# Turning values and decayed keys to token rows on VectorE instead of TensorE, in the head stage of a hybrid decoder layer

## The chip, the cores and the metric

The kernel runs on one core of a Trainium2 chip. The metric is the device time of one execution in microseconds, the median of several runs. One execution is also taken by the hardware profiler; its span (first to last instruction) and its rows are what the argument goes by.

## The reference

One step of a decoder layer with two branches over the same normalised tokens: HGRN2, a gated linear recurrence, and sliding-window attention. There are 1024 prompt tokens and 8 x 4 sample tokens, 1056 columns in all. The change lies in the recurrence, 8 heads of key and value width 128, computed chunk by chunk:

```python
b = jnp.cumsum(logf, axis=1)
...
o = jnp.einsum('bhts,bshv->bthv', att, v) + jnp.einsum('bthk,bhkv->bthv', q * jnp.exp(b), S)
b_last = b[:, -1]
k_dec = k * jnp.exp(b_last[:, None] - b)
S_new = jnp.exp(b_last)[..., None] * S + jnp.einsum('bshk,bshv->bhkv', k_dec, v)
```

q, k, v and the gates come from one projection of the tokens (1024 to 8448 columns). `k_dec` is the decayed key. Both `att @ v` and `k_dec^T v` sum over tokens, so v and `k_dec` are needed with tokens on the partitions.

## The kernel before

**Tiling.** The 1056 token columns are three slots of 352. A block is one 128-column tile of a weight matrix times all tokens; a slot of a block (L959, `slot`) is 24 matmuls into the PSUM bank `pj[g]`: eight tiles of the model width, each in three passes (weight high part with token high part, high with low, low with high), since fp32 is split into two fp32r parts. ScalarE makes a weight tile's high part (`split_hi`, L624), GpSimd its low part (`split_lo`, L554), SP loads it (`load`, L385) once the buffer is free. Projected blocks come out with channels on the partitions and tokens in the columns.

**The head stage.** It runs heads 0 to 7 (`head` on each engine, with a loop for 1 to 6). In head i, block 0 is the head's values, blocks 1, 2 and 3 are the next head's f, q and z, so that the next head's gates are computed meanwhile. Every engine has its order written out by hand, and the counts of its steps are kept by name in `Steps` tables (`act`, `dve`, `pe`, `pool`), so `dve.at(now, "dkm")` is the value that VectorE's semaphore has when step `dkm` of this head is done.

TensorE's order in a head: block 0 in three slots; block 1 slot 0; the transposes of the values (`vt0`, `vt1`, `vts`, nine) and of the decayed keys (`kt0`, `kt1`, `kts`, nine) with the identity as the moving operand (`turn`, L1025); block 1 slot 1; the intra-chunk products p0 and p1 (L1056 to L1071), which wait for VectorE's `dkm`; block 1 slot 2; `ps` and the eight products u (L1080) of `k_tok` and `v_tok`, which are the chunks' state updates; block 2 slots 0 and 1; the outputs o and `os` (L1087 to L1099), which wait for `atts`; block 2 slot 2; the sample tokens' state updates `us`; block 3 slot 0; the sums of squares `ms`; block 3 slots 1 and 2.

VectorE's order: `ha`, the norm of the head before (L1469); `kD`, the decayed key (L1473); four products into `d64` and `d32` (L1476, L1477); `dqm`, `dkm`, `qIm` (L1479 to L1482); the copies of the turned keys from PSUM to `k_tok` (L1485, L1487); the rounded parts of the sample tokens' keys `k3_hi`, `k3_hi2`, `k3_lo` (L1489 to L1492); the chain of states s1 to s8 (L1499, L1506); the masked scores `att0`, `att1`, `atts`; then the next head's exponents and the gates.

ScalarE copies the value slots from `pj` to `vT` (L705), which frees the bank for block 1, computes the exponentials, copies the turned values to `v_tok` (L729, L731) and rounds the sample tokens' part twice (L733, L734), for which GpSimd waits before `v3_lo` (L573) and `vexp` (L575).

Of the kernel before, what the change touches and what calls it, by code (L numbers as in the profile page):

```python
# [33 lines left out]
ACT = mybir.ActivationFunctionType  # L34

P = 128
# [4 lines left out]
NS = NB * DEC  # L41
T = SEQ + NS
NC = SEQ // P
SLOTS = 3
W = T // SLOTS
# [46 lines left out]
def hybrid_step(nc, x_prompt, x_sample, state_hgrn, cache_k, cache_v, norm_in, w_in, lb_logits, a_gnorm,  # L92
# [21 lines left out]
    norms = ["rl0", "rl1", "rls", "rx"]  # L114
    exponentials = ["v0", "ebl", "ebs", "xkD", "v1", "x64", "x32", "v2", "xdq", "xdk", "xqI"]
    turned = ["vt0", "vt1", "vts", "v3_hi", "v3_hi2"]
    squares_of_head = ["sq0", "sh0", "sq1", "sh1", "sqs", "shs"]
# [17 lines left out]
    exponents = ["kf", "scan", "kDa", "kDs", "a64q", "a64k", "a32q", "a32k", "cs", "css", "xa", "xas", "xc"]  # L135
    products = ["kD", "m64q", "m64k", "m32q", "m32k", "dqm", "dkm", "qIm", "kt0", "kt1", "kts", "k3_hi", "k3_hi2", "k3_lo"]
    chain = [f"s{c}" for c in range(1, NC + 1)]
# [20 lines left out]
    ])  # L158
    head_products = ["vt0", "vt1", "vts", "kt0", "kt1", "kts", "p0", "p1", "ps", "u0", "u1",
                     "o0", "o1", "os", "us0", "us1", "ms0", "ms1", "mss"]  # L160
# [18 lines left out]
    with ctx:  # L179
# [7 lines left out]
        pj = [ctx.enter_context(nc.psum_tensor(f"pj{g}", [P, 512], F32)) for g in range(SLOTS)]  # L187
        ps_a, ps_b, ps_c, ps_d, ps_e = [ctx.enter_context(nc.psum_tensor(f"ps_{n}", [P, 512], F32)) for n in "abcde"]
# [10 lines left out]
        ident = sb("ident", [P, P])  # L199
# [25 lines left out]
        k = sb("k", [P, T], where=area)  # L225
# [327 lines left out]
        def _(g):  # L553
# [11 lines left out]
            def head(i):  # L565
                B, now = head_blocks(i), now_of(i)
                split_lo(B(0))
                split_lo(B(1))
                if is_first(i):
                    g.wait_ge(masks_loaded, 48)  # L570
                g.wait_ge(act_done, act.at(now, "v3_hi2"))

                g.tensor_tensor(v3[NS:2 * NS, :], v_tok[0:NS, NC, :], v3[0:NS, :].bitcast(F32), ALU.subtract).then_inc(pool_done, pool.tick(now, "v3_lo"))  # L573
                g.wait_ge(pool_done, pool.at(now, "v3_lo"))
                g.tensor_tensor(v_exp[:], v3[:].bitcast(F32).rearrange("p (o v) -> p o v", o=1).to_broadcast([3 * NS, NB, P]),  # L575
                                batch_m[:].rearrange("p (b o) -> p b o", o=1).to_broadcast([3 * NS, NB, P]),
                                ALU.mult).then_inc(pool_done, pool.tick(now, "vexp"))
                split_lo(B(2))

                g.wait_ge(pe_done, pe.at(now, "os"))  # L580
                g.tensor_tensor(s0[:], s0[:], E[:, NC:NC + NB].rearrange("p (b o) -> p b o", o=1).to_broadcast([P, NB, P]),  # L581
                                ALU.mult).then_inc(pool_done, pool.tick(now, "s0e"))
                split_lo(B(3))
                if is_last(i):
                    split_lo(B(4))
# [34 lines left out]
        def _(a):  # L620
# [65 lines left out]
            def head(i):  # L686
# [15 lines left out]

                def v_copy(g):
                    a.wait_ge(slot_done, B(0)[0] * 3 + (g + 1))
                    a.activation(vT[:, span(g)], pj[g][:, 0:W], ACT.Copy).then_inc(act_done, act.tick(now, f"v{g}"))  # L705

                def exp(name, need, out, src, scale=1.0):
                    a.wait_ge(dve_done, dve.at(prev, need))
                    a.activation(out, src, ACT.Exp, scale=scale).then_inc(act_done, act.tick(now, name))

                v_copy(0)
                if not is_first(i):
# [3 lines left out]
                exp("xkD", "kDs", kD[:], kD[:])  # L716
                v_copy(1)
                exp("x64", "a64k", d64[:], d64[:])
                exp("x32", "a32k", d32[:], d32[:])
                v_copy(2)  # L720
                split_hi(B(2))
# [4 lines left out]
                exp("xqI", "scan", qI[:], b[:])  # L726
                for n, (bank, cols) in enumerate(((ps_a, slice(0, 4)), (ps_b, slice(4, 8)))):
                    a.wait_ge(pe_done, pe.at(now, f"vt{n}"))
                    a.activation(v_tok[:, cols, :], bank[:].rearrange("p (c v) -> p c v", c=4), ACT.Copy).then_inc(act_done, act.tick(now, f"vt{n}"))  # L729
                a.wait_ge(pe_done, pe.at(now, "vts"))  # L730
                a.activation(v_tok[0:NS, NC, :], ps_e[0:NS, 0:P], ACT.Copy).then_inc(act_done, act.tick(now, "vts"))  # L731
                a.wait_ge(act_done, act.at(now, "vts"))
                a.activation(v3[0:NS, :], v_tok[0:NS, NC, :], ACT.Copy).then_inc(act_done, act.tick(now, "v3_hi"))  # L733
# [222 lines left out]
        def _(t):  # L956
# [63 lines left out]
            def head(i):  # L1020
# [3 lines left out]

                def turn(bank, at, src, cols, name):  # L1025

                    for j, c in enumerate(cols):
                        r = P if c < NC else NS
                        mm = nc.tensor.transpose(bank[0:r, at + j * P:at + (j + 1) * P], src[:, c * P:c * P + r], ident[:, :])
                    mm.then_inc(pe_done, pe.tick(now, name))  # L1030

                def gate_slot(k_block, name, by, g):

                    if last and k_block == 3:
                        return
                    step = f"k{g}" if last and k_block == 2 else f"{name}{g}"
                    t.wait_ge(by[0], by[1].at(now, step))
                    slot(B(k_block), g)

                for g in range(SLOTS):  # L1040
                    t.wait_ge(dve_done, dve.at(prev, f"z{g}"))
                    slot(B(0), g)
                gate_slot(1, "v", (act_done, act), 0)
                t.wait_ge(act_done, act.at(now, "v2"))
                turn(ps_a, 0, vT, range(0, 4), "vt0")
                turn(ps_b, 0, vT, range(4, 8), "vt1")
                turn(ps_e, 0, vT, [NC], "vts")

                t.wait_ge(dve_done, dve.at(now, "kD"))
                turn(ps_c, 0, kD, range(0, 4), "kt0")  # L1050
                turn(ps_d, 0, kD, range(4, 8), "kt1")
                t.wait_ge(act_done, act.at(now, "vts"))
                turn(ps_e, P, kD, [NC], "kts")
                gate_slot(1, "v", (act_done, act), 1)

# [5 lines left out]
                for n, bank in enumerate((ps_a, ps_b)):  # L1061
# [9 lines left out]
                    mm.then_inc(pe_done, pe.tick(now, f"p{n}"))  # L1071
                gate_slot(1, "v", (act_done, act), 2)

                t.wait_ge(act_done, act.at(now, "vts"))
                t.wait_ge(dve_done, dve.at(now, "kts"))
                nc.tensor.matmul(ps_e[0:NS, 256:256 + NS], dk[:, SEQ:T], dq[:, SEQ:T], start=True, stop=True).then_inc(pe_done, pe.tick(now, "ps"))
# [272 lines left out]
        def _(v):  # L1349
# [106 lines left out]
            def head(i):  # L1456
# [4 lines left out]
                def need(steps, sem_, name):  # L1461
                    v.wait_ge(sem_, steps.at(now, name))

                def done(name):
                    return dve.tick(now, name)

                if not is_first(i):
                    need(act, act_done, "rx")
                    tt(ha[:, bass.ds(i - 1, 1), :], ha[:, bass.ds(i - 1, 1), :], rs[:].rearrange("p (o t) -> p o t", o=1), ALU.mult).then_inc(dve_done, done("ha"))  # L1469
                v.wait_ge(dve_done, dve.at(prev, "q2"))  # L1470

                need(act, act_done, "xkD")
                tt(kD[:], kD[:], k[:], ALU.mult).then_inc(dve_done, done("kD"))  # L1473
                for h, d in ((64, d64), (32, d32)):
                    need(act, act_done, f"x{h}")
                    tt(d[:, :, 1, :], d[:, :, 1, :], q[:, 0:SEQ].rearrange("p (c s t) -> p c s t", s=2, t=h)[:, :, 1, :], ALU.mult).then_inc(dve_done, done(f"m{h}q"))  # L1476
                    tt(d[:, :, 0, :], d[:, :, 0, :], k[:, 0:SEQ].rearrange("p (c s t) -> p c s t", s=2, t=h)[:, :, 0, :], ALU.mult).then_inc(dve_done, done(f"m{h}k"))  # L1477
                need(act, act_done, "xdk")
                tt(dq[:], dq[:], q[:], ALU.mult).then_inc(dve_done, done("dqm"))  # L1479
                tt(dk[:], dk[:], k[:], ALU.mult).then_inc(dve_done, done("dkm"))  # L1480
                need(act, act_done, "xqI")
                tt(qI[:], qI[:], q[:], ALU.mult).then_inc(dve_done, done("qIm"))  # L1482
                for n, bank in enumerate((ps_c, ps_d)):
                    need(pe, pe_done, f"kt{n}")
                    v.tensor_copy(k_tok[:, 4 * n:4 * n + 4, :], bank[:].rearrange("p (c v) -> p c v", c=4)).then_inc(dve_done, done(f"kt{n}"))  # L1485
                need(pe, pe_done, "kts")
                v.tensor_copy(k_tok[0:NS, NC, :], ps_e[0:NS, P:2 * P]).then_inc(dve_done, done("kts"))  # L1487
                need(dve, dve_done, "kts")
                v.tensor_copy(k3[0:NS, :], k_tok[0:NS, NC, :]).then_inc(dve_done, done("k3_hi"))  # L1489
# [280 lines left out]
```

## Time and profile before

| | us |
|---|---|
| median of 3 runs | 1321.42 (1320.48 to 1322.83) |
| the profiled execution, its own time | 1320.63 |
| its span | 1318.8 |
| TensorE busy (matmul) | 1287.5 |
| VectorE busy | 594.2 |
| ScalarE busy | 517.5 |
| GpSimd busy | 260.9 |
| mean granted TensorE clock over the span | 0.984 |

The busy shares add up what each engine did over the whole span. The chain is the work that ended last, followed back from the last instruction; what is not on it can move within its slack without moving the end. The timeline gives each instruction's start and duration and, in brackets, how long the engine was idle before it and what released it. The heads 1 to 6 repeat one pattern, so the rows of one of them stand for the others.

### The profile page before, as it was taken

How to read it: one execution, taken by the hardware profiler on the slowest of the kernel's cores; microseconds unless marked ns; L12 is line 12 of the kernel's file. 1: busy time of each engine (PE TensorE's matmuls, PEld its weight loads, DVE VectorE, ACT ScalarE, POOL GpSimd, SP SyncE). 2: the span in 40 equal slices, each digit the busy share in tenths (PEclk: the TensorE clock that was granted, in tenths of full speed). 3: DMA queues.
4: the chain of work that ended last, by engine and by line, in shares of the span. 5: the costliest groups of instructions: out<-in, count | busy, mean ns of one | idle time of the engine just before them, and what ended most of it. 6: DMA issues, size and time to landing. Idle time of an engine off the chain costs nothing.

```text
span 1318.8 us, 23470 instructions
## 1 busy us (share of the span) xinstructions
PE 1287.5 (98%) x9148; PEld 1227.6 (93%) x9148; DVE 594.2 (45%) x1237; ACT 517.5 (39%) x1019; POOL 260.9 (20%) x119
## 2 busy tenths in 40 slices
PE   5999999999999999999999999999999899999998
PEld 4999999999999999999999999999999899999885
DVE  6645657574847465600000155555556202345132
ACT  7463535445353535511111255555554324114111
POOL 0222221222322222222222111111110121342000
PEclk9999999999999999999999999999999899999999
DMA  6212121202021221121112311111100312241330
GB/s 198 67 33 66 36 65 34 80 18 80 18 80 37 76 58 41 35 64 48 48 35 49 85 33 32 32 32 32 32 16 1 106 32 64 62 98 33 119 125 37
DMA packets 136750, 73.61 MB, mean 56 GB/s; under 512 B 37185, under 2 KB 133138, under 8 KB 136690
## 3 DMA queue, kind: packets, MB, share of 16 engines
q1 hardware_dynamic: 136706, 72.99, 20.0%
q8 instruction: 31, 0.51, 0.2%
q14 instruction: 13, 0.11, 0.0%
HBM read 63.77 MB, written 10.22 MB: 56 GB/s over the span
## 4 chain that ended last, share of the span: by engine, by line
PE 93%; DVE 3%; ACT 2%; DMA 1%; issue 1%; SPq 0%; POOL 0%; DVEq 0%; ACTq 0%
PE pj L968 67%; PE pj L984 3%; PE pj L1328 3%; DVE scores L1617 2%; PE ps_a L1328 1%; PE ps_e L1328 1%; PE ps_d L1098 1%; PE ps_a L1169 1%; PE ps_d L1208 1%; PE ps_e L1208 1%; PE ps_b L1196 1%; PE ps_d L1328 1%; PE ps_b L1328 1%; PE ps_c L1328 1%; PE ps_c L1080 1%; PE ps_c L1196 1%
## 5 line engine op out<-in xcount | busy, mean ns | idle before, releaser
L968 PE MATMUL pj<-xn_h,w_h 128*128 128x352 f32 x1704 | 565.5, 332 | 3.4 <-DVE xn_l L1384 1.9
L968 PE MATMUL pj<-xn_h,w_l 128*128 128x352 f32 x1704 | 554.3, 325 | 0.0
L968 PE MATMUL pj<-xn_l,w_h 128*128 128x352 f32 x1704 | 553.5, 325 | 0.0
L558 POOL TENSOR_TENSOR w_l<-w_raw,w_h 128x1024 fp32r<-128x1024 f32 x82 | 203.3, 2479 | 688.8 <-ACT w_h L630 688.8
L968 PEld LDWEIGHTS pj<-xn_h,w_h 128*128 128x128 f32 x1704 | 325.8, 191 | 12.7 <-ACT w_h L630 3.5
L968 PEld LDWEIGHTS pj<-xn_l,w_h 128*128 128x128 f32 x1704 | 326.4, 192 | 0.3
L968 PEld LDWEIGHTS pj<-xn_h,w_l 128*128 128x128 f32 x1704 | 325.6, 191 | 0.0
L630 ACT ACTIVATE w_h<-w_raw 128x1024 fp32r<-128x1024 f32 x82 | 86.4, 1054 | 114.7 <-PE pj L968 100.1
L1565 DVE TENSOR_TENSOR mg<-sg,pj 128x352 f32 (+1 forms) x24 | 12.4, 522 | 151.9 <-PE pj L968 150.4
L835 ACT ACTIVATE scores<-scores,stat 128x256 f32<-128x256 f32 (+1 forms) x128 | 61.4, 481 | 0.0
L968 PE MATMUL pj<-hl_l,w_h 128*128 128x352 f32 x168 | 54.2, 323 | 0.0
L968 PE MATMUL pj<-hl_h,w_l 128*128 128x352 f32 x168 | 54.2, 323 | 0.0
L968 PE MATMUL pj<-hl_h,w_h 128*128 128x352 f32 x168 | 54.0, 321 | 0.0
L1399 DVE TENSOR_TENSOR zs<-zs,pj 128x352 f32<-128x352 f32 x24 | 12.5, 521 | 79.7 <-ACT zs L661 79.7
L581 POOL TENSOR_TENSOR s<-s,E 128x1024 f32<-128x1024 f32 x8 | 15.2, 1900 | 158.0 <-PE ps_d L1098 158.0
L661 ACT ACTIVATE zs<-pj 128x352 f32<-128x352 f32 x24 | 11.2, 465 | 84.7 <-PE pj L968 84.7
L949 ACT ACTIVATE y_sq<-y_o 128x1024 f32<-128x1024 f32 (+1 forms) x9 | 9.5, 1061 | 79.5 <-DVE y_o L1709 79.5
L1404 DVE TENSOR_TENSOR xn_l<-hb,xn_h 128x1056 fp32r<-128x1056 f32 x8 | 10.4, 1304 | 64.1 <-ACT xn_h L669 64.0
L661 ACT ACTIVATE sg<-pj 128x352 f32<-128x352 f32 x24 | 10.9, 465 | 66.7 <-PE pj L968 66.7
L1607 DVE TENSOR_SCALAR scores<-scores,stat 128x256 f32<-128x256 f32 (+1 forms) x128 | 35.5, 342 | 1.1
L1528 DVE TENSOR_TENSOR sq_l<-vT,sq_h 128x512 fp32r<-128x512 f32 (+1 forms) x24 | 33.6, 1451 | 0.0
L1687 DVE TENSOR_TENSOR sgb<-sgb,pj 128x352 f32 (+1 forms) x24 | 12.5, 520 | 46.7 <-PE pj L968 38.0
(362 smaller groups left out, 2005.4 us busy)
## 6 DMA issues: line engine op xcount, KB each, us to landing
w_raw<-in_w_in_dram SPq DMA_DIRECT2D x132, 256.0 KB, 3.4
x_t<-in_x_prompt_dram SPq DMA_DIRECT2D x8, 512.0 KB, 8.5
s<-in_state_hgrn_dram SPq DMA_DIRECT2D x8, 512.0 KB, 4.2
out_dram<-s SPq DMA_DIRECT2D x8, 512.0 KB, 3.2
w_raw<-in_w_pa_dram SPq DMA_DIRECT2D x16, 256.0 KB, 3.0
w_raw<-in_w_pb_dram SPq DMA_DIRECT2D x16, 256.0 KB, 4.5
wo_raw<-in_w_out_dram SPq DMA_DIRECT2D x8, 512.0 KB, 3.8
x_o<-in_x_prompt_dram SPq DMA_DIRECT2D x8, 512.0 KB, 4.1
```

Source lines behind the costliest of these rows:

```text
L558: g.tensor_tensor(w_l[p][:], w_raw[p][:], w_h[p][:].bitcast(F32), ALU.subtract).then_inc(w_lo_ready, 1)
L630: a.activation(w_h[p][:], w_raw[p][:], ACT.Copy).then_inc(w_hi_ready, 1)
L661: a.activation(out[:, span(g)], pj[g][:, 0:W], ACT.Sigmoid).then_inc(act_done, act.tick(where, f"{name}{g}"))
L835: a.activation(scores[:, u, keys], scores[:, u, keys], ACT.Exp, bias=stat[:, 1, u:u + 1], accum_out=stat[:, 3, u:u + 1]).then_inc(act_done ...
L968: mm = nc.tensor.matmul(pj[g][:, 0:W], w[:, kt, :], x[:, kt, span(g)], start=(kt == 0 and m == 0), stop=(kt == KT - 1 and m == 2))
L984: mm = nc.tensor.matmul(pj[g][:, 0:W], w[:, kt, :], x[:, kt, span(g)], start=(kt == 0 and m == 0), stop=(kt == KT - 1 and m == 2))
L1196: mm = nc.tensor.transpose(bank[:, o:o + P], scores[:, 2 * n + h, w * P:(w + 1) * P], ident[:, :])
L1208: mm = nc.tensor.matmul(bank[rows_h, o:o + P], v_tk[:, n - 1 + w, rows_h], PT[:, n % 3, 2 * h + w, :], start=(w == 0 or n == 0), stop=(w = ...
L1328: mm = nc.tensor.matmul(bank_of(n, m)[0:r, :], x[:, kt, cols], wo_rhs(m, lo, kt), start=(kt == 0 and i == 0), stop=(kt == KT - 1 and i == 2))
L1528: tt(sq_l[:, part[n]], vT[:, part[n]], sq_h[:, part[n]].bitcast(F32), ALU.subtract).then_inc(dve_done, done(f"sl{n}"))
L1607: v.tensor_scalar(target[:, u, keys(u)], target[:, u, keys(u)], st[:, 4, u:u + 1], None, ALU.mult).then_inc(dve_done, dve.tick(now, f"n{u}"))
L1617: v.tensor_tensor_reduce(out=scores[:, u, lo:2 * P], in0=bank[:, o + lo:o + 2 * P], in1=bias[:, h, lo:2 * P], scale=1.0, scalar=-3e38, op0 ...
```

## The change

TensorE no longer transposes in a head. VectorE does it with its 32x32 block transpose. For each value slot `turn_values(g)` reads the eleven 32-column blocks of `pj[g]` and writes them into `v_tok`; for each of the four value groups `iv` and four token groups `jt` one instruction turns all blocks of the slot that belong to that pair (two or three). The decayed keys are turned from `kD` in SBUF to `k_tok` in the same way, eight or nine blocks an instruction. `turn_values(0)` stands before `kD`, `turn_values(1)` after it, `turn_values(2)` after the products into `d64` and `d32`, and the keys after `qIm`. The copies of value slots to `vT` and of turned values on ScalarE and of turned keys on VectorE fall away. Block 1's slots now wait for the last transpose of a value slot (`v0_33`, `v1_33`, `v2_33`), and `ps` and u wait for `v2_33` and `kt33`. GpSimd's `v3_lo` gets a further wait, on the low part of block 1's weights.

```diff
-    exponentials = ["v0", "ebl", "ebs", "xkD", "v1", "x64", "x32", "v2", "xdq", "xdk", "xqI"]
-    turned = ["vt0", "vt1", "vts", "v3_hi", "v3_hi2"]
+    exponentials = ["ebl", "ebs", "xkD", "x64", "x32", "xdq", "xdk", "xqI"]
+    turned = ["v3_hi", "v3_hi2"]
...
                 g.wait_ge(act_done, act.at(now, "v3_hi2"))
+                g.wait_ge(w_lo_ready, B(1)[0] + 1)
...
-                v_copy(0)
...
-                v_copy(1)
...
-                v_copy(2)
...
-                for n, (bank, cols) in enumerate(((ps_a, slice(0, 4)), (ps_b, slice(4, 8)))):
-                    a.wait_ge(pe_done, pe.at(now, f"vt{n}"))
-                    a.activation(v_tok[:, cols, :], bank[:].rearrange("p (c v) -> p c v", c=4), ACT.Copy).then_inc(act_done, act.tick(now, f"vt{n}"))
-                a.wait_ge(pe_done, pe.at(now, "vts"))
-                a.activation(v_tok[0:NS, NC, :], ps_e[0:NS, 0:P], ACT.Copy).then_inc(act_done, act.tick(now, "vts"))
-                a.wait_ge(act_done, act.at(now, "vts"))
+                a.wait_ge(dve_done, dve.at(now, "v2_33"))
...
-                gate_slot(1, "v", (act_done, act), 0)
-                t.wait_ge(act_done, act.at(now, "v2"))
-                turn(ps_a, 0, vT, range(0, 4), "vt0")
-                turn(ps_b, 0, vT, range(4, 8), "vt1")
-                turn(ps_e, 0, vT, [NC], "vts")
-
-                t.wait_ge(dve_done, dve.at(now, "kD"))
-                turn(ps_c, 0, kD, range(0, 4), "kt0")
-                turn(ps_d, 0, kD, range(4, 8), "kt1")
-                t.wait_ge(act_done, act.at(now, "vts"))
-                turn(ps_e, P, kD, [NC], "kts")
-                gate_slot(1, "v", (act_done, act), 1)
+                gate_slot(1, "v", (dve_done, dve), 0)
+                gate_slot(1, "v", (dve_done, dve), 1)
...
-                gate_slot(1, "v", (act_done, act), 2)
-
-                t.wait_ge(act_done, act.at(now, "vts"))
-                t.wait_ge(dve_done, dve.at(now, "kts"))
+                gate_slot(1, "v", (dve_done, dve), 2)
+
+                t.wait_ge(dve_done, dve.at(now, "v2_33"))
+                t.wait_ge(dve_done, dve.at(now, "kt33"))
...
+                def turn_values(g):
+
+                    v.wait_ge(slot_done, head_blocks(i)(0)[0] * 3 + (g + 1))
+                    blocks = pj[g][:, 0:W].rearrange("p (b t) -> p b t", t=32)
+                    n = W // 32
+                    for iv in range(4):
+                        for jt in range(4):
+                            first = (jt - n * g) % 4
+                            c = (n * g + first) // 4
+                            many = len(range(first, n, 4))
+                            v.transpose(v_tok[32 * jt:32 * jt + 32, c:c + many, 32 * iv:32 * iv + 32],
+                                        blocks[32 * iv:32 * iv + 32, first:n:4, :]).then_inc(dve_done, done(f"v{g}_{iv}{jt}"))
+
                 if not is_first(i):
                     need(act, act_done, "rx")
                     tt(ha[:, bass.ds(i - 1, 1), :], ha[:, bass.ds(i - 1, 1), :], rs[:].rearrange("p (o t) -> p o t", o=1), ALU.mult).then_inc(dve_done, done("ha"))
+                turn_values(0)
                 v.wait_ge(dve_done, dve.at(prev, "q2"))
 
                 need(act, act_done, "xkD")
                 tt(kD[:], kD[:], k[:], ALU.mult).then_inc(dve_done, done("kD"))
+                turn_values(1)
...
+                turn_values(2)
                 need(act, act_done, "xdk")
...
-                for n, bank in enumerate((ps_c, ps_d)):
-                    need(pe, pe_done, f"kt{n}")
-                    v.tensor_copy(k_tok[:, 4 * n:4 * n + 4, :], bank[:].rearrange("p (c v) -> p c v", c=4)).then_inc(dve_done, done(f"kt{n}"))
-                need(pe, pe_done, "kts")
-                v.tensor_copy(k_tok[0:NS, NC, :], ps_e[0:NS, P:2 * P]).then_inc(dve_done, done("kts"))
-                need(dve, dve_done, "kts")
+                need(dve, dve_done, "kD")
+                key_blocks = kD[:].rearrange("p (b t) -> p b t", t=32)
+                for ik in range(4):
+                    for jt in range(4):
+                        many = NC + (jt == 0)
+                        v.transpose(k_tok[32 * jt:32 * jt + 32, 0:many, 32 * ik:32 * ik + 32],
+                                    key_blocks[32 * ik:32 * ik + 32, jt:4 * NC + (jt == 0):4, :]).then_inc(dve_done, done(f"kt{ik}{jt}"))
+                need(dve, dve_done, "kt33")
```

## Rows read from the trace of the kernel before

**Rows 1.** The page: TensorE's share, and the chain by engine.

```profile
PE 1287.5 (98%) x9148; PEld 1227.6 (93%) x9148; DVE 594.2 (45%) x1237; ACT 517.5 (39%) x1019; POOL 260.9 (20%) x119
...
PE 93%; DVE 3%; ACT 2%; DMA 1%; issue 1%; SPq 0%; POOL 0%; DVEq 0%; ACTq 0%
```

**Rows 2.** The chain in one head: start us, us, engine, tile, line, count.

```profile
189.99 14.80 PE pj L968 x93
204.79 0.44 PE ps_a L1029 x4
...
206.83 3.93 PE pj L968 x24
210.76 0.61 PE ps_a L1060 x8
...
212.97 4.01 PE pj L968 x24
216.98 0.18 PE ps_e L1076 x2
...
219.14 7.64 PE pj L968 x48
...
232.34 5.49 PE pj L968 x24
```

**Rows 3.** VectorE's timeline in the same head: start us, us, engine, line, operation.

```profile
194.04 1.26 DVE L1469 TENSOR_TENSOR ha<-ha,qI 128x1056 f32 x1 [3.48 <-ACT qI L698]
196.40 2.28 DVE L1473 TENSOR_TENSOR kD<-kD,k 128x1056 f32<-128x1056 f32 x1 [1.10 <-ACT kD L709]
198.64 0.69 DVE L1476 TENSOR_TENSOR d<-d,q 128x512 f32<-128x512 f32 x1
...
204.41 1.26 DVE L1479 TENSOR_TENSOR dq<-dq,q 128x1056 f32<-128x1056 f32 x1 [3.26 <-ACT dk L709]
205.58 1.25 DVE L1480 TENSOR_TENSOR dk<-dk,k 128x1056 f32<-128x1056 f32 x1
206.75 1.25 DVE L1482 TENSOR_TENSOR qI<-qI,q 128x1056 f32<-128x1056 f32 x1
207.92 0.69 DVE L1485 COPY k_tok<-ps_c 128x512 f32<-128x512 f32 x1
...
209.12 0.27 DVE L1487 COPY k_tok<-ps_e 32x128 f32<-32x128 f32 x1
209.42 3.27 DVE L1489 CAST k<-k_tok 32x128 fp32r<-32x128 f32 x1
212.73 0.22 DVE L1490 CAST k<-k_tok 32x128 fp32r<-32x128 f32 x1
212.97 0.28 DVE L1492 TENSOR_TENSOR k<-k_tok,k 32x128 fp32r<-32x128 f32 x1
218.28 0.29 DVE L1499 COPY S<-ps_c 128x128 f32<-128x128 f32 x1 [5.03 <-PE ps_c L1080]
...
222.61 0.17 DVE L1514 COPY_PREDICATED att_s<-causal_s,ps_e 32x32 f32<-32x32 int32 x1
```

**Rows 4.** GpSimd's timeline in the same head.

```profile
194.91 2.66 POOL L558 TENSOR_TENSOR w_l<-w_raw,w_h 128x1024 fp32r<-128x1024 f32 x1 [14.61 <-ACT w_h L630]
207.24 1.07 POOL L573 TENSOR_TENSOR v<-v_tok,v 32x128 fp32r<-32x128 f32 x1 [9.68 <-ACT v L734]
208.40 1.90 POOL L575 TENSOR_TENSOR v_exp<-v,batch_m 96x1024 fp32r<-96x1024 f32 x1
210.26 2.36 POOL L558 TENSOR_TENSOR w_l<-w_raw,w_h 128x1024 fp32r<-128x1024 f32 x1
```

**Rows 5.** A stretch of the same head: busy us, granted clock, DMA share, GB/s.

```profile
233.30:234.30 1.00, 1.00 (x5) 0.50 0.00 0
```

**Rows 6.** Head 0: ScalarE's timeline, the first copy of a value slot.

```profile
70.55 0.47 ACT L705 ACTIVATE vT<-pj 128x352 f32<-128x352 f32 x1 [0.98 <-PE pj L968]
```

**Rows 7.** Head 0: the chain at `ps`.

```profile
94.04 0.18 PE ps_e L1076 x2
```

More of the change, by code:

```diff
@@ L135, in hybrid_step @@
     exponents = ["kf", "scan", "kDa", "kDs", "a64q", "a64k", "a32q", "a32k", "cs", "css", "xa", "xas", "xc"]
-    products = ["kD", "m64q", "m64k", "m32q", "m32k", "dqm", "dkm", "qIm", "kt0", "kt1", "kts", "k3_hi", "k3_hi2", "k3_lo"]
+    turned_keys = [f"kt{i}{j}" for i in range(4) for j in range(4)]
+    turned_values = lambda g: [f"v{g}_{i}{j}" for i in range(4) for j in range(4)]
+    products = turned_values(0) + ["kD"] + turned_values(1) + ["m64q", "m64k", "m32q", "m32k"] + turned_values(2) + ["dqm", "dkm", "qIm"] + turned_keys + ["k3_hi", "k3_hi2", "k3_lo"]
     chain = [f"s{c}" for c in range(1, NC + 1)]
@@ L158, in hybrid_step @@
     ])
-    head_products = ["vt0", "vt1", "vts", "kt0", "kt1", "kts", "p0", "p1", "ps", "u0", "u1",
+    head_products = ["p0", "p1", "ps", "u0", "u1",
                      "o0", "o1", "os", "us0", "us1", "ms0", "ms1", "mss"]
@@ L701, in head @@
                 split_hi(B(1))
-                def v_copy(g):
-                    a.wait_ge(slot_done, B(0)[0] * 3 + (g + 1))
-                    a.activation(vT[:, span(g)], pj[g][:, 0:W], ACT.Copy).then_inc(act_done, act.tick(now, f"v{g}"))
                 def exp(name, need, out, src, scale=1.0):
@@ L1023, in head @@
                 last = is_last(i)
[L1025 to L1030, printed above, removed]
                 def gate_slot(k_block, name, by, g):
@@ L1035, in gate_slot @@
                         return
-                    step = f"k{g}" if last and k_block == 2 else f"{name}{g}"
+                    step = f"k{g}" if last and k_block == 2 else f"v{g}_33" if name == "v" else f"{name}{g}"
                     t.wait_ge(by[0], by[1].at(now, step))
```

## The prediction

> **What bounds the kernel now.** I read three things in this order: the page's busy shares with its chain, the chain of work of one head in order of time, and VectorE's and GpSimd's timelines of that same head. TensorE is busy for 98% of the span and carries 93% of the chain [rows 1], so only time taken from TensorE, or a new wait of TensorE, moves the end. The chain of one head (the one whose first projection slot begins at about 189.5 us) shows no wait at all: slots of 24 projection matmuls follow each other, with the small head products between them [rows 2]. So the reader is to see TensorE's program order as a timetable: block 0 (values) up to 200.97, block 1 slot 0 up to 204.79 (48 matmuls, two slots, take 7.64, so 3.82 a slot), the 18 transposes up to 206.83, block 1 slot 1 up to 210.76, the intra-chunk products p (which need `dkm`) up to 212.97, block 1 slot 2 up to 216.98, then `ps` and the state products u (which need `kts`, the last turned key) [rows 2]. Against it stands VectorE's timetable: `ha` ends at 195.30, it has `dkm` at 206.83 and the last key copy at 209.39 [rows 3], 3.9 and 7.6 us before TensorE asks for them. That is the slack of this kernel, and it is what the change spends.
>
> **What is removed.** 18 transposes, from 204.79 to 206.83: 2.04 us of TensorE per head, all on the path [rows 2], 8 x 2.04 = 16.3 us. If nothing else moved, the profiled execution's 1320.6 us would become 1304.3. ScalarE loses its three copies of value slots and three of turned values; it is not on the path, so this is worth nothing. VectorE loses two key copies at 0.60 each from start to start and one of 0.27 [rows 3].
>
> **What is added.** 64 VectorE transposes per head. A value slot has 11 blocks of 32 columns: 12 instructions of 96 elements and 4 of 64 per partition, three slots. The keys are 12 instructions of 256 and 4 of 288. Per head that is 3 x 1408 + 4224 = 8448 elements over 64 instructions, 132 each. No row shows a 32x32 transpose, so I build its price.
>
> Rate: copies from PSUM of 128 and of 512 columns take 0.29 and 0.69, so 384 more elements cost 0.39 to 0.40, 1.04 ns each; an SBUF product of 1056 takes 1.26, which leaves a fixed part of 0.16, and the copies leave 0.16 too (0.14 for the one on 32 partitions) [rows 3]. I take 0.15. A block's first transposed row can only leave when its last column of 32 is in, 32 x 1.04 = 0.033, since that is what transposing means; whether it is paid is unknown.
>
> Spacing: ordinary neighbours overlap, 1.26 us products start 1.17 apart, 0.09 less than they last [rows 3]. But look at the two rounding copies `k3_hi` and `k3_hi2`, with no wait between them: the second writes partitions 32 to 63 after the first wrote 0 to 31, and starts at 212.73 where the first ended at 212.69; the next, which writes 64 to 95, starts at 212.97 after 212.95 [rows 3]. So where the 32-partition group of the output changes, the overlap is gone and some 0.03 us is added. The new loops step `jt` innermost, so the output's group changes at each of the 64. I take spacing = duration + 0.03.
>
> The Trainium skill (VectorE: DVE Perf Modes, section "Two Vector instructions with no wait between them") has the general form: an instruction starts only after all earlier ones have finished if its input or output begins in another 32-partition quadrant than the last one from or to that memory. The trace agrees in the pairs just read; by that rule all 64 would be held, as I assume, while by the ordinary overlap of this trace the 64 would cost 64 x 0.12 = 7.7 us less per head. The same page (section "The three transpose paths") gives 311 ns for a VectorE transpose of 128x128 bf16; by it an estimate of the fixed part is 0.18, and no run here shows it.
>
> Price by rows: 96 elements 0.100 + 0.15 + 0.033 + 0.03 = 0.313; 64 elements 0.280; 256 elements 0.480; 288 elements 0.513. One value slot 12 x 0.313 + 4 x 0.280 = 4.88 us, the keys 12 x 0.480 + 4 x 0.513 = 7.81. Together 3 x 4.88 + 7.81 = 22.4 us per head. Lower end: no block latency, 0.14 fixed: 2.8 less, 19.7. Lower still if nothing is held: 14.8, or 12.0 with both. Upper end: fill and drain of a block both paid, 2.1 more, 24.5.
>
> **Where it lies.** VectorE's order in the shown head becomes: `ha` to 195.2 | values 0 to 200.1 | `kD` 1.17 to 201.3 (it lasts 2.28 now because GpSimd's subtraction runs to 197.57 [rows 3, 4]; after it, it lasts 1.26) | values 1 to 206.2 | four products of 0.60 to 208.6 | values 2 to 213.5 | `dqm`, `dkm` to 215.8 | `qIm` to 217.0 | keys to 224.8. Without the transposes these fixed pieces end at 202.3. So there are two thresholds: if the 64 take up to 12.6 us (0.197 each), TensorE keeps its whole 2.04; at 14.7 us (0.229 each) `kt33` comes at 216.98 and nothing is won; each us beyond is lost.
>
> TensorE: block 1 slot 1 now waits for `v1_33` (206.2 against 204.8), ends at 210.05, then TensorE stands idle for `dkm` until 215.8; p to 218.0, slot 2 to 221.9, wait for `kt33` until 224.8. The u products start at 224.8 in place of 216.98: +7.8 us. Does a slow clock add to it? After the thin products that end at 232.34 the granted clock is 0.50 (1.2 GHz), and the slot behind them takes 5.49 in place of 3.8 [rows 2, 5]. An idle stretch of 5.8 us is thinner work than those, so p (2.2, at half speed 4.4) and slot 2 (5.5) could end at 225.7, 0.9 past `kt33`. I take +8.0 for the head.
>
> Who waits behind? TensorE's queue is in order, so block 2 and the next head's block 0 move with u. Behind u all is as now: the state chain and the masks follow u and end 222.61 + 0.17 = 222.8, while TensorE asks for `atts` at 219.14 + 7.64 = 226.78, 4 us later [rows 2, 3]. Also `k3` costs 3.27 now because GpSimd holds it up [rows 3, 4]; it becomes 0.2, and it has no reader that waits. ScalarE's sigmoids of block 1 wait for `qIm` (217.0 in place of 208.0), but block 2 slot 0 starts only after u. GpSimd's new wait on `w_lo_ready` of B(1) is for its own earlier subtraction: nothing. SP's weight loads follow GpSimd's `w_lo`, some us later, behind a timetable that is itself 8 us later: nothing.
>
> Head 0 has no `ha`: slot 0's copy starts at 70.55 and u at 94.04 [rows 6, 7]. 70.5 + 22.4 + 7.1 = 100.0, +6.0. Sum: 7 x 8.0 + 6.0 = 62 us; 1320.6 + 62 = 1382.6 for the profiled execution, which lies 0.8 under the median of 1321.4. Forecast: 1383 us.
>
> **Rivals.**
> (a) The transposes overlap as ordinary instructions do: 12.0 to 14.8 us for the 64. At 12.0 all 2.04 are kept, 1305; at 14.8 nothing, 1322. It decides from 0.229 us per transpose downwards. For it: none of the rows is a transpose, and no row has a PSUM input whose group changes. Against it: the `k3` pairs, which show the same gap in every head. Chance 0.14, of which 0.10 end faster and 0.04 within 0.2%.
> (b) GpSimd and VectorE collide. `kD` and the `k3` copy show that SBUF work of VectorE waits until GpSimd's run of instructions is over, and GpSimd's `v3_lo` takes 1.07 where its 128 columns at the rate of the 1024-column subtraction would be 0.3 [rows 3, 4]. `v3_lo` moves to about 214, beside `dqm`, `dkm`, `qIm`; `vexp` (1.90) and the subtraction of block 2 (2.36) follow [rows 4]. If `dkm` or `qIm` waits for `vexp`: +1.9; if the key transposes wait for the subtraction too: +4.3. The copies from PSUM at 207.92 to 209.39 ran beside GpSimd unhindered [rows 3, 4], so the values are safe; the keys, SBUF to SBUF, are not shown. With +1.9 to +4.3 per head, or a dearer transpose (+2.1): 1398 to 1433. Chance 0.24.
> (c) The hold is there but the fixed part is small (19.7 us): u at 222.1 to 223, +5 to +6: 1361 to 1368. It is the low end of the forecast, and counted with it.
> (d) The clock loses more: TensorE is still at half speed in u and block 2, as after the thin products, another 1.7 per head: 1396. Counted with (b)'s range, chance 0.05.
>
> **How the numbers follow.** Forecast with (c): 0.53, own range 1358 to 1397. (b) and (d) together 0.29. (a) 0.14. Something between no change and 1358, from a hold that costs less than the pairs show: 0.04. The range 1352 to 1428 leaves out (a), most of that last case and the top of (b), together about 0.2. Faster by over 0.2% 0.10, within 0.2% 0.05, slower by over 0.2% 0.85; 0.2% is about what a measurement of this kernel can tell from no change.
>
> **What would show it.** In the new profile: VectorE transposes of 0.28 to 0.31 us (values) and 0.45 to 0.5 (keys) that start after the one before has ended; 22 us of them per head; a head longer by 8 us; TensorE idle before p of some 6 us and before `ps` of up to 3 us, released by VectorE; a granted clock of 0.5 around p. The prediction is wrong if transposes start 0.2 us or less apart, since TensorE then never waits, or if they cost 0.45 us and more for 96 elements, since 1430 is then passed.

## The result and the profile after

The changed kernel takes 1430.27 us (median of 4 runs, 1428.83 to 1431.41), the kernel before 1321.99 beside it: ratio 1.082, 95% interval 1.0801 to 1.0839. The loss is 108 us; the forecast was 62 us (1383), with a range up to 1428, so the result lies 2 us above its top.

The page of the changed kernel, its busy shares, its chain by engine and by line, and the groups of VectorE's lines that the change touches, with shapes apart (busy us, mean ns):

```profile
PE 1306.2 (91%) x9004; PEld 1243.9 (87%) x9004; DVE 749.8 (52%) x1725; ACT 497.9 (35%) x971; POOL 266.2 (19%) x119
...
PE 71%; DVE 19%; issue 6%; ACT 3%; POOL 1%; DMA 0%; SPq 0%; ACTq 0%; DVEq 0%; POOLq 0%
```

```profile
L1451 DVE STREAM_TRANSPOSE v_tok<-pj 32x96 f32<-32x96 f32 x288 | 80.3, 279 | 11.5 <-PE pj L959 2.8
L1472 DVE TENSOR_TENSOR qI<-qI,q 128x1056 f32<-128x1056 f32 x8 | 42.2, 5269 | 0.0
L1478 DVE STREAM_TRANSPOSE k_tok<-kD 32x256 f32<-32x256 f32 x96 | 41.9, 437 | 3.0
...
L1451 DVE STREAM_TRANSPOSE v_tok<-pj 32x64 f32<-32x64 f32 x96 | 23.7, 247 | 3.0
...
L1478 DVE STREAM_TRANSPOSE k_tok<-kD 32x288 f32<-32x288 f32 x32 | 14.9, 465 | 0.7
```

VectorE, which was 3% of the chain [rows 1], is now 19% of it. A transpose costs what was forecast. But `qIm`, which took 1.25 [rows 3], takes 5.27 in every head. VectorE's timeline of one head, to set against [rows 3]:

```profile
221.58 1.26 DVE L1456 TENSOR_TENSOR ha<-ha,qI 128x1056 f32 x1 [3.48 <-ACT qI L701]
222.76 4.80 DVE L1451 STREAM_TRANSPOSE v_tok<-pj 32x96 f32<-32x96 f32 x16
227.58 1.26 DVE L1461 TENSOR_TENSOR kD<-kD,k 128x1056 f32<-128x1056 f32 x1
228.87 4.80 DVE L1451 STREAM_TRANSPOSE v_tok<-pj 32x96 f32<-32x96 f32 x16
...
241.06 1.26 DVE L1469 TENSOR_TENSOR dq<-dq,q 128x1056 f32<-128x1056 f32 x1
242.24 1.51 DVE L1470 TENSOR_TENSOR dk<-dk,k 128x1056 f32<-128x1056 f32 x1
243.67 5.27 DVE L1472 TENSOR_TENSOR qI<-qI,q 128x1056 f32<-128x1056 f32 x1
248.87 7.57 DVE L1478 STREAM_TRANSPOSE k_tok<-kD 32x288 f32<-32x288 f32 x16
```

GpSimd's timeline in the same stretch, to set against [rows 4]:

```profile
241.78 0.85 POOL L576 TENSOR_TENSOR v<-v_tok,v 32x128 fp32r<-32x128 f32 x1 [16.66 <-ACT v L725]
242.71 2.79 POOL L578 TENSOR_TENSOR v_exp<-v,batch_m 96x1024 fp32r<-96x1024 f32 x1
245.47 2.36 POOL L560 TENSOR_TENSOR w_l<-w_raw,w_h 128x1024 fp32r<-128x1024 f32 x1
```

The row of `qIm` is 5.27 long, but the product itself takes 1.25 [rows 3], so it stood still for 4.0: its end, 248.94, lies 1.1 behind the end of GpSimd's subtraction (245.47 + 2.36 = 247.83), which had followed `vexp` without a gap (242.71 + 2.79 = 245.50). `dkm` lost only 0.26, to `v3_lo` (1.51 against 1.25): it went ahead in the gap between `v3_lo` and `vexp` (242.63 to 242.71), and `vexp` then lost 0.9 to it (2.79 against 1.90). What TensorE waited for, in the whole execution (us in total, times, longest):

```profile
PE ps_a L1034 <- DVE dk L1470: 47.7, 8, 6.0
PE ps_e L1050 <- DVE k_tok L1478: 34.0, 8, 5.1
PE pj L959 <- DVE v_tok L1451: 9.7, 7, 1.4
```

TensorE's busy time and granted clock in stretches of that head: the wait for `dkm`; the products p; block 1 slot 2; the wait for `kt33`; `ps` and u; the slot behind o and `os`:

```profile
237.70:243.70 6.00, 0.12 (x1) 0.73 0.00 0
243.70:247.90 4.20, 4.10 (x114) 0.57 0.00 0
247.90:251.60 3.70, 3.70 (x24) 1.00 0.49 142
251.70:256.40 4.70, 0.00 (x0) 0.76 0.00 0
256.50:260.50 4.00, 4.00 (x19) 0.50 0.00 0
...
274.00:279.50 5.50, 5.50 (x25) 0.69 0.00 0
```

There are three stretches at the low level (0.50 is 1.2 GHz) in place of one: after each of the two idle stretches, and behind o and `os` as before. `ps` and u, 2.16 us before (216.98 to 219.14 [rows 2]), take 4.03.

### The profile page after: what moved, and what is told of

It reads as the page before. It is cut to its first block, busy times and chain, and to the rows that moved or that the text cites. A ratio compares the mean times of both kernels' runs of the same rounds, so it can differ in the third digit from the quotient of the medians.

```text
span 1428.8 us, 23587 instructions
## 1 busy us (share of the span) xinstructions
PE 1306.2 (91%) x9004; PEld 1243.9 (87%) x9004; DVE 749.8 (52%) x1725; ACT 497.9 (35%) x971; POOL 266.2 (19%) x119
## 4 chain that ended last, share of the span: by engine, by line
PE 71%; DVE 19%; issue 6%; ACT 3%; POOL 1%; DMA 0%; SPq 0%; ACTq 0%; DVEq 0%; POOLq 0%
PE pj L959 48%; DVE v_tok L1451 7%; DVE k_tok L1478 3%; PE pj L975 3%; DVE qI L1472 3%; PE pj L1302 2%; DVE scores L1609 2%; PE ps_a L1302 1%; PE ps_e L1302 1%; PE ps_e L1182 1%; PE ps_a L1143 1%; PE ps_d L1182 1%; PE ps_c L1054 1%; PE ps_d L1072 1%; PE ps_b L1170 1%
## 5 line engine op out<-in xcount | busy, mean ns | idle before, releaser
L1451 DVE STREAM_TRANSPOSE v_tok<-pj 32x96 f32<-32x96 f32 (+1 forms) x384 | 104.0, 271 | 14.5 <-PE pj L959 2.8
L826 ACT ACTIVATE scores<-scores,stat 128x256 f32<-128x256 f32 (+1 forms) x128 | 61.4, 481 | 0.0
L1478 DVE STREAM_TRANSPOSE k_tok<-kD 32x256 f32<-32x256 f32 (+1 forms) x128 | 56.8, 444 | 3.8
L1034 PE MATMUL ps_a<-d 128*64 128x64 f32 x64 | 8.9, 321 | 47.7 <-DVE dk L1470 47.7
L1034 PEld LDWEIGHTS ps_a<-d 128*64 128x64 f32 x64 | 7.4, 222 | 50.0 <-DVE dk L1470 50.0
L1472 DVE TENSOR_TENSOR qI<-qI,q 128x1056 f32<-128x1056 f32 x8 | 42.2, 5269 | 0.0
L664 ACT ACTIVATE q<-pj 128x352 f32<-128x352 f32 x24 | 11.2, 466 | 86.5 <-PE pj L959 86.5
```

The costliest lines, as they stand in the source:

```text
L826: a.activation(scores[:, u, keys], scores[:, u, keys], ACT.Exp, bias=stat[:, 1, u:u + 1], accum_out=stat[:, 3, u:u + 1]).then_inc(act_done ...
L1034: nc.tensor.matmul(bank[0:64, o + 64:o + 128], d64[:, c, 0, :], d64[:, c, 1, :], start=True, stop=True)
L1451: v.transpose(v_tok[32 * jt:32 * jt + 32, c:c + many, 32 * iv:32 * iv + 32], blocks[32 * iv:32 * iv + 32, first:n:4, :]).then_inc(dve_done ...
L1478: v.transpose(k_tok[32 * jt:32 * jt + 32, 0:many, 32 * ik:32 * ik + 32], key_blocks[32 * ik:32 * ik + 32, jt:4 * NC + (jt == 0):4, :]).the ...
```

## The experiments

Eight kernels ran. Ratios are to the kernel before, with 95% intervals.

**1. GpSimd held back until `qIm` is done.**

```diff
                 g.wait_ge(w_lo_ready, B(1)[0] + 1)
+                g.wait_ge(dve_done, dve.at(now, "qIm"))
```

> The changed kernel with one wait more: GpSimd's v3_lo (and with it vexp and the subtraction for block 2) starts after VectorE's qIm. Theory A (the qIm product of 5.27 us stands still behind GpSimd's vexp and w_l, and that is the part of the loss that I mis-sized): qIm takes 1.25 us, the key transposes start 4.0 us earlier, the u products too; 8 x 4.0 = 32 us less, about 1398 us. Theory B (transposes from SBUF to SBUF wait for GpSimd as well): GpSimd's 0.3 + 1.9 + 2.4 us now lie beside the key transposes, one of them shows several us, and the time stays at about 1430.

Measured: 1377.57 us (1375.67 to 1381.05), ratio 1.0426 (1.0407 to 1.0446), 52.7 us less than the changed kernel. VectorE's and GpSimd's timelines of a head:

```profile
228.05 1.25 DVE L1471 TENSOR_TENSOR dk<-dk,k 128x1056 f32<-128x1056 f32 x1
229.22 1.25 DVE L1473 TENSOR_TENSOR qI<-qI,q 128x1056 f32<-128x1056 f32 x1
230.39 7.58 DVE L1479 STREAM_TRANSPOSE k_tok<-kD 32x288 f32<-32x288 f32 x16
```

```profile
230.55 0.45 POOL L577 TENSOR_TENSOR v<-v_tok,v 32x128 fp32r<-32x128 f32 x1 [19.64 <-DVE qI L1473]
231.08 1.89 POOL L579 TENSOR_TENSOR v_exp<-v,batch_m 96x1024 fp32r<-96x1024 f32 x1
232.93 2.38 POOL L560 TENSOR_TENSOR w_l<-w_raw,w_h 128x1024 fp32r<-128x1024 f32 x1
```

`qIm` is back at 1.25. GpSimd's three instructions now lie beside the key transposes, and neither side grows (7.58 against 7.57; 1.89 and 2.38): theory B falls. The gain is 20 us more than theory A's 32. TensorE's stretches show where it is: the wait for `dkm`, the products p, block 1 slot 2, `ps` with u, and the slot behind o and `os`:

```profile
223.60:229.30 5.70, 0.02 (x1) 0.85 0.00 0
229.30:233.50 4.20, 4.14 (x113) 0.50 0.00 0
233.50:238.00 4.50, 4.27 (x24) 0.90 0.27 79
238.00:240.20 2.20, 2.18 (x19) 1.00 0.26 77
...
253.50:257.40 3.90, 3.90 (x25) 1.00 0.00 0
```

TensorE's waits for `kt33` fall from 34.0 us in all to 1.4. With the second idle stretch gone, u runs at full clock again. So a late `kt33` costs twice: its own lateness, and TensorE's slow products after it.

**2. The two loops of the transposes swapped**, so that the output's partition group changes at every fourth instruction only and the input's at each (keys likewise).

```diff
-                    for iv in range(4):
-                        for jt in range(4):
+                    for jt in range(4):
+                        for iv in range(4):
```

> The changed kernel with the two loops of the transposes swapped: the output's 32-partition group now changes only at every fourth instruction, the input's at each. Theory A (a change of the output group alone holds an instruction back, as I read it from the k3 pairs): 48 of the 64 transposes overlap again, 0.12 us each, 5.8 us less per head, about 1384 us. Theory B (a change of the input group holds it just as much, by the Trainium skill's rule): all 64 stay 0.31 and 0.47 us apart, 1430 us, within 0.2%.

Measured: 1430.17 us (1429.99 to 1430.77), ratio 1.0816 (1.0798 to 1.0834). A slot of values still takes 4.80 from first start to last end, the keys 7.57. Theory B stands: a change of the input's group holds as much as one of the output's.

**3. The keys alone on VectorE**, after `qIm`, with the change's own loop; the values stay on TensorE.

```diff
-                t.wait_ge(dve_done, dve.at(now, "kD"))
-                turn(ps_c, 0, kD, range(0, 4), "kt0")
-                turn(ps_d, 0, kD, range(4, 8), "kt1")
-                t.wait_ge(act_done, act.at(now, "vts"))
-                turn(ps_e, P, kD, [NC], "kts")
                 gate_slot(1, "v", (act_done, act), 1)

+                t.wait_ge(act_done, act.at(now, "vts"))
                 t.wait_ge(dve_done, dve.at(now, "dkm"))
...
-                t.wait_ge(dve_done, dve.at(now, "kts"))
+                t.wait_ge(dve_done, dve.at(now, "kt33"))
```

> The kernel before with the keys alone turned on VectorE (after qIm, as in the change); the values stay on TensorE. TensorE loses 1.07 us of transposes per head. Theory A (VectorE's slack of 7.6 us before ps carries the keys and nothing carries the values): VectorE turns the keys in 7.6 us from about 207.95 to 215.5 of the head in the rows, TensorE is at ps at 215.9, no wait: 8 x 1.07 = 8.5 us less than before, about 1313 us. Theory B (the key transposes wait for GpSimd, which is busy to 212.6): they end near 220, ps waits 4 us, about 1346 us.

Measured: 1310.33 us (1308.66 to 1310.47), ratio 0.9905 (0.9888 to 0.9921): faster than the kernel before by 12 us. One head, VectorE and then GpSimd:

```profile
205.91 1.25 DVE L1478 TENSOR_TENSOR qI<-qI,q 128x1056 f32<-128x1056 f32 x1
207.08 7.58 DVE L1484 STREAM_TRANSPOSE k_tok<-kD 32x288 f32<-32x288 f32 x16
```

```profile
206.40 1.07 POOL L573 TENSOR_TENSOR v<-v_tok,v 32x128 fp32r<-32x128 f32 x1 [9.68 <-ACT v L734]
207.56 1.89 POOL L575 TENSOR_TENSOR v_exp<-v,batch_m 96x1024 fp32r<-96x1024 f32 x1
209.41 2.38 POOL L558 TENSOR_TENSOR w_l<-w_raw,w_h 128x1024 fp32r<-128x1024 f32 x1
```

Here too the transposes run beside GpSimd at their full pace, and TensorE never waits for them. Of the 12 us, 8.5 are the nine transposes (1.07 x 8). A head's period goes from 61.4 to 60.0 on average, 1.4 in place of 1.07, and the trace shows where the other 0.3 comes from: four of the six periods are 60.2 to 60.35, the transposes' share; in the other two, 59.5, the slot behind o and `os` takes 3.9 in place of 5.47, because the granted clock stays up (TensorE then waits 0.5 for GpSimd's weights at the next slot). One stretch of each kind:

```profile
192.90:253.00 60.10, 60.10 (x483) 0.97 0.20 53
253.00:313.00 60.00, 59.47 (x489) 1.00 0.20 54
```

Why it stays up in some heads, these runs don't show. The two profiled executions are 10.2 us apart (spans 1308.6 and 1318.8), the medians 12.3.

**4. The same with eight of the sixteen key transposes before `dqm`.**

```diff
-    products = ["kD", "m64q", "m64k", "m32q", "m32k", "dqm", "dkm", "qIm", "kt0", "kt1", "kts", "k3_hi", "k3_hi2", "k3_lo"]
+    products = (["kD", "m64q", "m64k", "m32q", "m32k"] + [f"kt{i}{j}" for i in range(2) for j in range(4)] + ["dqm", "dkm", "qIm"]
+                + [f"kt{i}{j}" for i in range(2, 4) for j in range(4)] + ["k3_hi", "k3_hi2", "k3_lo"])
```

> As the run with the keys alone, but eight of the sixteen key transposes stand before dqm, where VectorE is idle for 3.3 us, and eight after qIm. Theory A: dkm comes 0.6 us later than before and is still 2.4 us early, kt33 at about 212.3, no wait of TensorE: about 1313 us, the same as the keys alone within 0.2%. Theory B (the keys wait for GpSimd): the second eight end near 216.4, ps waits 0.5 us, about 1317 us.

Measured: 1310.0 us (1309.49 to 1310.49), ratio 0.9905 (0.9889 to 0.9922). The same as the run before, as theory A had it: the keys lie inside VectorE's slack in either place.

**5. The values alone on VectorE**, the keys on TensorE between block 1 slots 0 and 1.

```diff
-                need(dve, dve_done, "kD")
-                key_blocks = kD[:].rearrange("p (b t) -> p b t", t=32)
...
+                for n, bank in enumerate((ps_c, ps_d)):
+                    need(pe, pe_done, f"kt{n}")
+                    v.tensor_copy(k_tok[:, 4 * n:4 * n + 4, :], bank[:].rearrange("p (c v) -> p c v", c=4)).then_inc(dve_done, done(f"kt{n}"))
```

> The other half alone: the values are turned on VectorE as in the change, the keys stay on TensorE and are copied from PSUM as before. Theory A (the values set the loss, because their 14.5 us stand in front of dkm): dkm comes as late as in the changed kernel, TensorE stands idle some 6 us before p and is at ps about when it is in the run with GpSimd held back; 1375 to 1385 us. Theory B (values and keys each carry their share of VectorE's time): the keys' 7.6 us are saved, 4 to 6 us per head less than that, 1335 to 1345 us.

Measured: 1374.77 us (1373.14 to 1375.69), ratio 1.0401 (1.0383 to 1.0418): theory A, a hair under its window. `qIm` takes 5.26 here as well, but behind it come only the key copies, and no wait of TensorE at `ps` is left. What it waits for:

```profile
PE ps_a L1045 <- DVE dk L1481: 46.8, 8, 6.0
```

So the values alone cost 52.5 us, and the late `qIm` costs nothing where nothing late stands behind it. In a head TensorE starts p 5.6 us later than in the kernel before, and p with block 1 slot 2 takes 8.2 in place of 6.2, because p runs at the low clock: +7.5 at `ps`, where run 1, which has the keys' 7.6 us of VectorE besides, has +7.8. So two paths of nearly the same length lead to `ps` in run 1: over `dkm` and the slow p, and over `kt33`. Shortening one alone gains nearly nothing.

**6. Transposes by themselves**, 44 of them with 64 elements, behind the last step of the kernel before; their results are not used.

```diff
+            for src in (sbuf, psum):
+                turn_some(src, [(0, 32, 0)] * 6)
+                turn_some(src, [(0, 32, o) for o in (1, 2, 3, 0, 1, 2)])
+                turn_some(src, [(a, 32, 2) for a in (1, 2, 3, 0, 1, 2)])
+                turn_some(src, [(0, P, 0)] * 4)
```

(Each triple: the input's first group, partitions, the output's first group.)

> The kernel before with 44 VectorE transposes of 64 elements added behind the last step, where nothing else runs; from SBUF and then from PSUM: six within partitions 0 to 31, six whose output group changes, six whose input group changes, four over all 128 partitions. Their results are used by nothing. Theory A (the hold comes from a change of either group): the first six and the 128-partition ones start 0.15 to 0.17 us apart, the others 0.27 to 0.28. Theory B (a transpose always waits for the one before it to drain): all start 0.27 to 0.28 apart. The time grows by the 10 us or so of the added work.

The chain of that stretch, where an entry of several runs to the end of its last:

```profile
1316.70 0.87 DVE sgb L1722 x6
1317.57 0.01 issue
1317.58 0.23 DVE sgb L1722
1317.81 0.01 issue
...
1319.07 0.24 DVE sgb L1722
...
1320.58 1.40 DVE sgb L1722 x10
```

And the timeline in short windows that move on by one instruction within the first six; the first number is the start of the earliest in the window:

```profile
1316.87 0.32 DVE L1722 STREAM_TRANSPOSE sgb<-g_fin 32x64 f32<-32x64 f32 x2
1316.99 0.44 DVE L1722 STREAM_TRANSPOSE sgb<-g_fin 32x64 f32<-32x64 f32 x3
1317.12 0.45 DVE L1722 STREAM_TRANSPOSE sgb<-g_fin 32x64 f32<-32x64 f32 x3
```

Within one group the transposes start 0.126 apart (0.17 the first time). The six together take 0.87, 0.145 each, only because that time holds the last one's full length. Each one whose output's or input's group changes starts 0.25 after the one before. The last entry is ten together: four over all 128 partitions, again 0.126 apart, and the first six from PSUM, 0.13 apart; the held ones from PSUM are 0.25 to 0.27 apart. Theory A, with prices 0.02 to 0.03 lower than expected. A change of group so costs 0.12 us. The one time of this kernel was 1327.79 us, 5.5 above the kernel before where some 10 had been expected; the reading is the spacing, not the time.

**7. GpSimd's weight subtraction ahead of `v3_lo` and `vexp`.**

```diff
                 if is_first(i):
                     g.wait_ge(masks_loaded, 48)
+                split_lo(B(2))
                 g.wait_ge(act_done, act.at(now, "v3_hi2"))
-                g.wait_ge(w_lo_ready, B(1)[0] + 1)
+                g.wait_ge(w_lo_ready, B(2)[0] + 1)
...
-                split_lo(B(2))
```

> The changed kernel with GpSimd's subtraction for block 2 (2.4 us) moved ahead of v3_lo and vexp, so that less of GpSimd's run stands against qIm. Theory A (qIm waits until GpSimd's unbroken run is over): qIm takes about 2.9 us in place of 5.3, ps comes 2.4 us earlier, 8 x 2.4 = 19 us less, about 1411 us, and less again if the slow clock at u goes. Theory B (qIm is slow for a reason of its own): 1430 us.

Measured: 1407.52 us (1406.07 to 1409.05), ratio 1.0642 (1.0625 to 1.066). In VectorE's timeline `qIm` is shorter by 2.3, about the subtraction's 2.4:

```profile
237.96 2.94 DVE L1472 TENSOR_TENSOR qI<-qI,q 128x1056 f32<-128x1056 f32 x1
```

Theory A. The loss follows the length of GpSimd's run: 2.3 us a head are 18.6 of the 22.8 us gained. TensorE's waits for `kt33` fall from 34.0 us in all to 18.1, and `ps` with u is slow for its whole length in some heads, for part of it in others and in one not at all.

**8. Run 1 with the values of slot 2 turned behind `qIm`.**

```diff
-                turn_values(2)
                 need(act, act_done, "xdk")
...
                 tt(qI[:], qI[:], q[:], ALU.mult).then_inc(dve_done, done("qIm"))
+                turn_values(2)
```

> The run with GpSimd held back, and the values of slot 2 turned behind qIm in place of before dqm. Theory A (what sets a head is the sum of VectorE's work ahead of kt33, wherever the wait of TensorE lies): dkm comes 4.8 us earlier and the idle stretch before p shrinks from 5.7 to 1 us, but block 1 slot 2 then waits 4 us for v2_33 and ps 4 us for kt33; the time is the same 1377 us or, if the slow clock reaches u, up to 1395. Theory B (the late dkm sets it): 4 us less per head, about 1345 us.

Measured: 1381.81 us (1380.14 to 1382.87), ratio 1.0452 (1.0435 to 1.047), 4 us above run 1. The waits of TensorE:

```profile
PE pj L960 <- DVE v_tok L1452: 39.5, 15, 3.7
PE ps_e L1051 <- DVE k_tok L1479: 11.4, 8, 2.0
...
PE ps_a L1035 <- DVE dk L1470: 5.9, 8, 0.8
```

Theory A: the wait for `dkm` shrinks from 45.7 us in all to 5.9, and turns up again at `v2_33` and `kt33`. The three waits add up to 56.8 us here and in run 1 (45.7 + 9.7 + 1.4). Moving values behind `dkm` shortens the first of run 5's two paths and leaves the second: the sum of VectorE's work ahead of `kt33` is the same, and so is the start of `ps` (30.6 us after `ha` in both runs). The 4 us more are the slow clock: in three of the eight heads u takes 3.3 to 3.5 in place of 2.05.

## Why the prediction was wrong

**Bound and direction: right.** TensorE's program order against VectorE's timetable was the frame that held. The two thresholds (12.6 us for no wait, 14.7 for no change) put the 64 transposes, at 22 us, on the losing side. Runs 3 to 5 confirm the slack from the other side: 7.6 us of keys fit into it, 14.5 us of values don't. Both thresholds are those of `kt33`; the values have a tighter one, at `dkm`, which the prediction does not name. By its own rows VectorE's fixed pieces end there at 201.1 and TensorE asks at 210.76, so 9.7 us of values are free of loss (7.6 with the transposes' 2.04 kept), and 14.5 are not, with or without keys (run 5).

**Price of a transpose: right.** Forecast 0.313, 0.280, 0.480 and 0.513 from start to start. Measured durations 0.279, 0.247, 0.437 and 0.465, plus the 0.03 between them: 0.31, 0.28, 0.47 and 0.50. A slot of values took 4.83 (forecast 4.88), the keys 7.6 (7.81). The hold on a change of partition group was there at each (runs 2 and 6). The rule of the Trainium skill (VectorE: DVE Perf Modes, "Two Vector instructions with no wait between them") that input and output count alike is borne out; the `k3` pairs had shown only the output side. Without the hold, at 0.126 in place of 0.25, each would cost 0.124 less (run 6), 7.9 us per head, where rival (a) had 7.7. By that estimate the 64 would take 22.1 - 7.9 = 14.2, between the two thresholds and just under no change. So the hold decides between the loss and about no change; that is worked out, not run.

**The head without collisions: right.** Run 1 is the forecast's own model, with `qIm` at 1.25. From the `ha` product to `ps` it needs 30.7 us where the kernel before needs 22.9: +7.8, as forecast. Its period is 68.8 against 61.4 (412.7 and 368.5 us over six heads), +7.4 where +8.0 was forecast: the 0.2 for slow products p did not come, and the slow slot behind o and `os` went away in four of the six. Its time of 1377.6 is 5 us under the forecast of 1383.

**The term that failed** is the one that was put at nothing in the sum: "Where it lies", with `dkm` to 215.8 and `qIm` to 217.0, taken at 1.17 each. The collision stood among the rivals as (b), with 0.24, and the sum left it out. It was +4.0 at `qIm` and +0.26 at `dkm`, 4.3 us per head; (b) had +1.9 if `qIm` waits for `vexp`, and +4.3 only if the key transposes wait for the subtraction too. In fact `qIm` waited for `vexp` and the subtraction, and the key transposes for neither: the size of (b)'s upper price is met, but by another path, which is luck. The rows of before held the pattern: the `k3` copy asked at 209.42, while `vexp` ran, and came through only after the subtraction that followed it [rows 3, 4]. Where GpSimd's next instruction follows without a gap, as the subtraction behind `vexp` (245.47 against 245.50), it goes ahead of the waiting VectorE one. In the gap of 0.08 before `vexp`, `dkm` went first. Reading it so gives 1.9 + 2.4 at `qIm`.

The Trainium skill (SBUF — State Buffer, "SBUF: two separate sides") says that a VectorE instruction with two SBUF inputs, or in a two-port mode, and a GpSimd one exclude each other for a whole instruction, and others don't. The trace agrees: the products, with two inputs, waited; the transposes, with one, never did (runs 1 and 3). One input alone is not what spares an instruction: the `k3` copy has one, and took 3.27 in the kernel before [rows 3] and 0.21 where GpSimd was idle (256.47 in the changed kernel). That its mode is the reason, no run here shows.

**The clock: found, but one place short.** Forecast was a slow stretch at p, hidden by `kt33`; it came and was all but hidden in run 1. Rival (d), slow products u, had 0.05 and was counted apart from (b). They are not apart: the collision makes the second idle stretch (4.9 us before `ps`), and the slow u follows from it. On average per head, from run 1 to the changed kernel (68.8 to 75.4): 4.2 for the late `kt33`, 1.6 for slow `ps` and u (3.6 against 2.0 from the start of `ps` to that of block 2), and 0.8 from there to the next head, where the slow slot behind o and `os` comes in all six heads and in only two of run 1's. That makes 6.6, 53 us over eight heads, the difference measured.

**Range.** Its top of 1428 lies between what (b) gives alone and what the two rivals give together. (b) at its dearest, +4.3 per head, is 1383 + 34 = 1417; the 1433 that the prediction names takes the dearer transpose as well. (d)'s 1.7 per head on top makes 1431. (b) with its companion (d) is the case that happened, at 14.0 us per head over the kernel before.

## What to carry to other kernels

Weigh the work that moves to another engine against that engine's slack before the bound engine's next question, and count its instructions, not only its elements: 48 value transposes of some 0.3 us did not fit into the slack, 16 key transposes with the same number of elements in all, three times as many each, did. Moving the keys alone is the version that beats both kernels, 1310 us. When an instruction moves, look at what now runs beside each of its neighbours on VectorE and GpSimd, and take the whole gapless run of the other engine as the wait, not one instruction of it. Where a late wait follows thin work on TensorE, add the slow products after it to its price instead of keeping the two as separate cases.

## What the runs showed of the hardware that was not expected

VectorE transposes of 64 columns over all 128 partitions start 0.126 us apart, no more than those over 32 partitions in a single group, while one that changes group starts 0.25 after the last (run 6). So a change of group costs some 0.12 us on instructions this short, as much as the instruction itself.

A VectorE product that met a gapless run of GpSimd's instructions waited for all of them: 5.27, 2.94 and 1.25 us for the same product with two, one and none of them left in front of it (the changed kernel, runs 7 and 1).

The slow clock behind o and `os`, a slot of 5.49 in place of 3.8 [rows 2], is worth less than it looks. In run 1's head it is absent, and the slot takes 3.9, 1.6 less. But from the end of u to the next head's `ha` pass 35.6 us, against 36.4 in the kernel before, only 0.8 less: TensorE waits at the next slot for GpSimd's weights instead (4.6 us of window, 4.07 busy). In two of run 1's six periods the slow slot is there (5.5), and these last 69.2 and 69.4 against 68.3 to 68.8. In the head without it:

```profile
257.40:262.00 4.60, 4.07 (x25) 1.00 0.11 32
```
